# A three-layer block network on one core: tiles placed a round ahead, the modulation in five pieces over three layers, delta masks made with the update

## The reference

```python
for l in range(2):                                   # layers 0 and 1
    shift, scale, gate = split(silu(c) @ w_ada[l] + b_ada[l], 3)     # the modulation, 2048 x 6144
    h = rms_norm(x, norm_g[l]) * (1 + scale) + shift
    u, z_s, q, k, v, z_a = split(h @ w_in[l])        # 6 x 1024 columns
    y_s = s5_mixer(u, ...) * silu(z_s)               # 64 groups of 64 complex states, a scan over time
    y_a = diff_attention(rope(q), rope(k), v, ...) * silu(z_a)       # 8 heads of two maps
    x = x + gate * (concat(y_s, y_a) @ w_out[l])
x = rms_norm(x, final_g)
# layer 2
shift, scale, gate = split(silu(c_2) @ w_ada_2 + b_ada_2, 3)
h = rms_norm(x, norm_gain_2) * (1 + scale) + shift
q_a, k_a, v_a, z_a, b_a, a_a, q_b, k_b, v_b, z_b, gl_a, gl_b = split(h @ w_in_2)
q_a, k_a, v_a = silu(conv4(q_a, k_a, v_a))           # q_a, k_a then of unit length per head
o_a = gated_delta_rule_chunked(q_a, k_a, v_a, g(a_a), sigmoid(b_a))  # 8 heads, chunks of 64 tokens
o_b = sliding_window_attention(q_b, k_b, v_b, ...)   # 16 heads, window 128
mixed = sigmoid(gl_a) * (o_a' @ w_branch_gdn) + sigmoid(gl_b) * (o_b' @ w_branch_swa)
out = x + gate * (mixed @ w_out_2)
```

## Time and profile before

| | us |
|---|---|
| median of 3 runs (lowest, highest) | 4688.14 (4687.24, 4689.46) |
| the profiled execution's own time | 4688.89 |
| its span in the profile | 4687.1 |
| TensorE busy in it | 4429.2 |
| VectorE, ScalarE, GpSimd busy | 1940.2, 818.5, 484.1 |

### The profile page before, as it was taken

One profiled execution on the slowest core, in us unless ns is written; L12 is line 12 of the kernel. 1 busy time (PEld: TensorE's weight loads), 2 busy tenths in 40 slices (PEclk: granted clock), 3 DMA queues, 4 the chain that ended last, 5 costly groups with the idle time before them and its releaser, 6 DMA issues.

```text
span 4687.1 us, 34250 instructions
## 1 busy us (share of the span) xinstructions
PE 4429.2 (94%) x13238; PEld 2253.4 (48%) x13238; DVE 1940.2 (41%) x3496; ACT 818.5 (17%) x1384; POOL 484.1 (10%) x802
## 2 busy tenths in 40 slices
PE   7898899999889989999999899989899999999999
PEld 3454444444436545444444355555555554444444
DVE  4555535664543454356545535151514223321100
ACT  1122201231002221011300212120211013330000
POOL 0122211111321231101022000000000000000000
PEclk8999999999999999999999989999999999999999
DMA  8422233335472222322357321211121222223332
GB/s 295 171 90 74 92 109 104 115 120 169 151 239 79 86 72 83 110 88 68 108 190 233 127 81 36 69 49 59 47 70 48 92 72 68 67 88 128 99 103 76
DMA packets 366736, 495.17 MB, mean 106 GB/s; under 512 B 43899, under 2 KB 277870, under 8 KB 365550
## 3 DMA queue, kind: packets, MB, share of 16 engines
q1 hardware_dynamic: 288112, 340.16, 22.1%
q0 software_dynamic: 37632, 122.71, 8.2%
q10 hardware_dynamic: 40830, 30.11, 2.0%
HBM read 460.42 MB, written 32.51 MB: 105 GB/s over the span
## 4 chain that ended last, share of the span: by engine, by line
PE 75%; DVE 13%; DMA 6%; ACT 2%; issue 2%; ACTq 1%; POOL 0%; DVEq 0%; SPq 0%; POOLq 0%
PE bank L108 73%; DMA side<-in_w_ada 5%; DVE tring L123 4%; DVE tring L117 2%; PE bank L111 2%; ACT tring L114 1%; ACTq L147 1%; DVE tring L132 1%; DVE tring L120 1%; DVE CA L117 1%; DVE SS L117 1%; DVE tring L144 1%; DVE tb L117 1%; DVE dring L120 0%; ACT Est L114 0%
## 5 line engine op out<-in xcount | busy, mean ns | idle before, releaser
L108 PE MATMUL bank<-region_b,wring 128*128 128x512 f32 x4160 | 1872.5, 601 | 9.7 <-ACT region_b L114 9.7
L108 PEld LDWEIGHTS bank<-region_b,wring 128*128 128x128 f32 x4160 | 780.6, 193 | 904.6 <-issue 895.9
L108 PE MATMUL bank<-region_a,wring 128*128 128x512 f32 x2048 | 914.1, 601 | 10.8 <-DMA wring<-in_w_out 10.8
L108 PEld LDWEIGHTS bank<-region_a,wring 128*128 128x128 f32 x2048 | 387.8, 193 | 475.1 <-issue 473.7
L123 DVE SCALAR_TENSOR_TENSOR tring<-side,cact,tring 128x512 f32<-128x512 f32 x420 | 343.2, 817 | 218.1 <-DMA side<-in_w_ada 184.2
L147 POOL DMA_DIRECT2D side<-in_w_ada x448 | 242.8, 542 | 1499.2 <-DVE tring L123 976.5
L114 ACT ACT_TABLE_LOAD x196 | 251.5, 1283 | 437.9 <-DVE sring L120 285.4
L108 PE MATMUL bank<-wring,region_b 128*128 128x512 f32 (+2 forms) x768 | 285.4, 527 | 0.0
L132 DVE RECIPROCAL tring<-tring 128x512 f32<-128x512 f32 x54 | 180.7, 3348 | 134.1 <-ACT tring L114 134.0
L108 PE MATMUL bank<-wring,region_a 128*128 128x512 f32 x512 | 226.4, 600 | 5.9 <-ACT region_a L114 5.9
L108 PE MATMUL bank<-yaT,wring 128*128 128x512 f32 x512 | 227.3, 597 | 0.0
(11 more groups left out here) (237 smaller groups left out, 3320.7 us busy)
## 6 DMA issues: line engine op xcount, KB each, us to landing
wring<-in_w_in SPq DMA_DIRECT2D x180, 1024.0 KB, 5.2
side<-in_w_ada POOLq DMA_DIRECT2D x448, 256.0 KB, 3.2
wring<-in_w_out SPq DMA_DIRECT2D x48, 1024.0 KB, 7.4
yaT<-in_w_ada SPq DMA_DIRECT2D x16, 1024.0 KB, 7.2
wring<-in_w_glu SPq DMA_DIRECT2D x16, 1024.0 KB, 7.8
tring<-x_saved SPq DMA_DIRECT2D x48, 256.0 KB, 3.6
SS<-in_w_ada SPq DMA_DIRECT2D x8, 1024.0 KB, 8.3
side<-in_w_ada SPq DMA_DIRECT2D x8, 1024.0 KB, 9.1
```

Source lines behind the costliest of these rows:

```text
L108: return self.e.matmul(*a, **k) if self.e else self
```

## The change

1. `e_place` of round k+1 is written ahead of `scan` of round k, and `bc_place` of round k into round k instead of k+1.
2. The modulation is five pieces: gate of layer 0, shift and scale of layer 1, gate of layer 1, shift and scale of layer 2, and gate of layer 2, the last beside the window attention of layer 2 through four slots of its own (`gring`). The rates of `carry` go from 1.0, 1.5 and 4 (layer 0) and 0.5, 0.8 and 4 (layer 1) in the three stages of a layer to 1.25, 1.7 and 1.8 in both, and 1.6 in the window attention; `finish_behind` leaves 3 and 2 pieces in layer 0, and 1 and 0 in layer 1.
3. In `state_space_params(1)` two more steps pass between the fetch and the first use.
4. The delta rule's mask for n+1 is made right after the update of n, and one step more lies before n = 1. The separate VectorE step `d_lo` is gone.
5. The convolution has two input tiles (`raws`) instead of one, and its second half, `conv_rest`, is a step later than its first; the unit chain starts a step later still.
6. `ba` is one tile with its 16 columns as weights: 16 matmuls with 512 tokens, a copy on ScalarE, four turns, and the gates made from the turned tile in one instruction each.
7. In the last layer each four channel tiles of the output are turned, copied and stored as soon as they are made (`leave`): 16 stores of 256 KB instead of four of 1 MB.

```diff
@@ -527,7 +530,11 @@
-        mods = [(0, [SHIFT, SCALE]), (0, [GATE]), (1, [SHIFT, SCALE, GATE]), (2, [SHIFT, SCALE, GATE])]
+        mods = [(0, [SHIFT, SCALE]), (0, [GATE]), (1, [SHIFT, SCALE]), (1, [GATE]), (2, [SHIFT, SCALE]), (2, [GATE])]
+        GATE_OF = [1, 3, 5]
...
+        def ada_slots(m):
+            return wide_slots if m == GATE_OF[2] else mslots
...
@@ -704,7 +711,8 @@
-            yield
+            for _ in range(3 if l else 1):
+                yield
...
@@ -728,10 +736,8 @@
             for k in range(NK + 1):
-                if k < NK:
+                if k == 0:
                     do("e_place", l, k)
-                if k:
-                    do("bc_place", l, k - 1)
                 yield
...
@@ -757,6 +763,9 @@
                     aux.give("y", l, k - 1)
+                if k < NK:
+                    do("bc_place", l, k)
+                if k:
                     yield
...
@@ -765,6 +774,8 @@
                     aux.give("y_turn", l, k - 1)
+                if k < NK - 1:
+                    do("e_place", l, k + 1)
                 if k < NK:
...
@@ -879,6 +890,18 @@
+        def leave(k0):
...
+            yield
+            for j in range(TT):
+                aux.take("o_turn", j, k0)
+                do("o_turn", j, k0)
+                aux.give("o_turn", j, k0)
+                if j % 2:
+                    yield
+            for j in range(TT):
+                do("o_store", j, k0)
...
@@ -888,14 +911,14 @@
-                    return None
+                    return leave(n + j - 3) if l == 2 and (n + j) % 4 == 3 else None
...
-            carried[0] = [1.0, 0.5][l]
+            carried[0] = 1.25
...
@@ -911,7 +934,7 @@
-                behind.extend([modulation(1), modulation(2), modulation(3)])
+                behind.extend([modulation(m) for m in range(1, 5)])
...
@@ -920,13 +943,13 @@
-            carried[0] = [1.5, 0.8][l]
+            carried[0] = 1.7
...
-            finish_behind(2 - l)
-            carried[0] = 4
+            finish_behind(3 - 2 * l)
+            carried[0] = 1.8
...
@@ -934,7 +957,7 @@
-            finish_behind(1 - l)
+            finish_behind(2 - 2 * l)
...
@@ -956,15 +979,14 @@
-            def unit():
+            yield
+            do("conv_rest", h0, which, j)
+            yield
+            if which < 2:
...
-                temps.give("conv", h0, which, j)
...
-            if which < 2:
-                return unit()
...
-            return None
...
@@ -1152,7 +1175,12 @@
-        run_all(dense(layer_dense(2, w_two, OFF["ba"], "keep_ba", tokens="blocks", n=2 * GH)))
+        temps.take("ba")
+        run_all(dense(layer_dense(2, w_two, OFF["ba"], "keep_ba", n=2 * GH)))
+        aux.take("ba_turn")
+        do("ba_turn")
+        aux.give("ba_turn")
+        temps.give("ba")
...
@@ -1165,19 +1193,17 @@
+        behind.append(modulation(GATE_OF[2]))
+        carried[0] = 1.6
...
+        finish_behind(0)
...
+        do("fence", "mixed")
...
-        do("fence", "end")
-        for j in range(TT):
-            for k0 in range(0, KT, 4):
-                aux.take("o_turn", j, k0)
-                do("o_turn", j, k0)
-                aux.give("o_turn", j, k0)
-            do("o_store", j)
+        run_all(settle())
...
@@ -2149,17 +2186,20 @@
-                dve.memset(raw[:, 0:3], 0.0).then_inc(*delta_d.up("raw"))
+                dve.memset(raws[:, :, 0:3], 0.0).then_inc(*delta_d.up("raw"))
...
-                c, acc = HT * which + h0 + j, temps.at("conv", h0, which, j)
+                c, acc, raw = HT * which + h0 + j, temps.at("conv", h0, which, j), raws[:, j, :]
...
-                for i in range(1, 4):
-                    own()
-                    dve.scalar_tensor_tensor(acc, raw[:, i:i + T], convw[:, i, c:c + 1], acc, M, AD).then_inc(
-                        *(taken_d.up("conv", h0, which, j) if i == 3 else d_step.up()))
+                stt(acc, raw[:, 1:1 + T], convw[:, 1, c:c + 1], acc, M, AD)
...
+            def conv_rest(h0, which, j):
+                c, acc, raw = HT * which + h0 + j, temps.at("conv", h0, which, j), raws[:, j, :]
+                stt(acc, raw[:, 2:2 + T], convw[:, 2, c:c + 1], acc, M, AD)
+                own()
+                dve.scalar_tensor_tensor(acc, raw[:, 3:3 + T], convw[:, 3, c:c + 1], acc, M, AD).then_inc(*taken_d.up("conv", h0, which, j))
...
@@ -2251,11 +2291,7 @@
-            def d_lo(h, n):
-                if n > 1:
-                    dve.wait_ge(*delta_full.of("dm", h, n - 1))
-                join(h, n)
+                join(h, 1)
...
@@ -2265,6 +2301,8 @@
                 aux.leave(("d_dt", h, n), dve.mine())
+                if n < 5:
+                    join(h, n + 1)
...
@@ -2701,8 +2739,16 @@
+                room(temps.clear("ba"))
...
-                act.activation(gates[:, 1, j, :], banks.at(jid, j)[:, 0:GH], ACT.Sigmoid).then_inc(*taken_a.up("ba", j))
+                act.activation(temps.at("ba")[0:2 * GH, :], banks.at(jid, j)[0:2 * GH, :], ACT.Copy).then_inc(*taken_a.up("ba_tile"))
+                banks.leave((jid, j), act.mine())
...
+            def ba_turn():
+                bank = aux.at("ba_turn")[:, 0:2 * GH * TT].rearrange("p (j h) -> p j h", j=TT)
+                act.wait_ge(*turned.of("ba"))
+                act.activation(gates[:, 1, :, :], bank[:, :, 0:GH], ACT.Sigmoid).then_inc(*taken_a.up("ba"))
+                aux.leave(("ba_turn",), act.mine())
...
@@ -2717,12 +2763,14 @@
-                prev = (h0, which, j - 1) if j else (h0, which - 1, 1) if which else (h0 - 2, 2, 1)
+                prev = (h0, which - 1, j) if which else (h0 - 2, 2, j)
...
-                act.activation(raw[:, 3:T + 3], banks.at(jid, j)[:, :], ACT.Copy).then_inc(*delta_a.up("raw", h0, which, j))
+                act.activation(raws[:, j, 3:T + 3], banks.at(jid, j)[:, :], ACT.Copy).then_inc(*delta_a.up("raw", h0, which, j))
...
+            def conv_rest(h0, which, j):
...
@@ -2997,11 +3045,10 @@
-            def o_store(j):
+            def o_store(j, k0):
...
-                for k0 in range(0, KT, 4):
-                    sp.wait_ge(*(taken_a if k0 % 8 else taken_d).of("o", j, k0))
-                sp.dma_start(out[0, j * P:(j + 1) * P, :], row).then_inc(*out_stored.landing(j))
+                sp.wait_ge(*(taken_a if j % 2 else taken_d).of("o", j, k0))
+                sp.dma_start(out[0, j * P:(j + 1) * P, k0 * P:(k0 + 4) * P], row[:, k0 * P:(k0 + 4) * P]).then_inc(*out_stored.landing(j, k0))
...

```

More of the change, by code:

```diff
@@ L315, in build @@
         band, k2, q2 = sb("band", [P, 16, 256], two), sb("k2", [P, 2, T], two), sb("q2", [P, 2, T], two)
+        gring = sb("gring", [P, 4, T], two)
         two.close()
@@ L324, in build @@
         wslots, mslots = Room([wring[:, i, :, :] for i in range(4)]), Room([mring[:, i, :, :] for i in range(3)])
+        wide_slots = Room([gring[:, i, :].unsqueeze(1) for i in range(4)])
         temps = Room([tring[:, i, :] for i in range(NTEMP)])
@@ L337, in build @@
         ada_in = [sem(f"ada_in{i}") for i in range(3)]
+        late_ada_in = [sem(f"late_ada_in{i}") for i in range(4)]
         first_in = [sem(f"first_ada_in{i}") for i in range(4)]
@@ L503, in fetch @@
                     c = todo.pop(0)
-                    mslots.take("ada", m, *c)
+                    ada_slots(m).take("ada", m, *c)
                     do("ada_fetch", m, *c)
-            for _ in range(len(mslots.places)):
+            for _ in range(len(ada_slots(m).places)):
                 fetch()
@@ L1456, in band_ @@
                           stop=True).then_inc(*scored.up("band", h))
+            def ba_turn():
+                bank, ba = aux.at("ba_turn"), temps.at("ba")
+                room(aux.clear("ba_turn"))
+                pe.wait_ge(*taken_a.of("ba_tile"))
+                for j in range(TT):
+                    i = pe.transpose(bank[:, 2 * GH * j:2 * GH * (j + 1)], ba[0:2 * GH, J[j]], ident[0:2 * GH, 0:2 * GH])
+                i.then_inc(*turned.up("ba"))
+                temps.leave(("ba",), pe.mine())
             def gate_sums():
```

55 lines of the change are left out of this document (29 added, 26 removed).

## The result

The changed kernel takes 4568.01 us (median of 4, 4566.52 to 4569.43), the one before 4688.39 (4 runs, 4687.24 to 4689.46): the ratio is 0.9744, with a 95% interval of 0.973 to 0.9758. It is faster by 120 us, where 177 were forecast, and it lies 18 us outside the range of 4475 to 4550.

A forecast was written before the change was run, and what follows sets the result against it. TensorE was taken to set the time, with savings from its idle time and clock. Terms 80 + 42 + 8 + 20 + 29 + 2 - 1 - 3 = 177 us off gave 4511 us against the 4688.1 median; range 4475 to 4550.

The forecast's parts named there:

- The step that failed: Window attention of layer 2: 64 modulation sums beside it, mostly covered by TensorE's work, cost 1 us (0 to 8).
- rival (d): State space and attention: the modulation's DMA waits move onto the path with 333 sums; 4690 us or more; chance 0.03.
- state space: State-space stages: 14 of 16 waits for `Est` go, 62 us, plus 18 of clock; 80 us (60 to 91).
- output products of both layers, less the rate's cost: Output stages gain 42 and 8 us, mainly from waits tied to modulation's pace; attention loses 3 to the rate.
- opening of layer 2: Opening of layer 2: wide `ba` saves 11 us, waits and clock the rest; 20 us (6 to 26).
- delta rule: Delta rule: masks directly after updates cut TensorE's waits, with 5 us of clock; 29 us (10 to 50).
- end: Kernel's end: turns only move, but fewer bytes remain after the last store; 2 us (0 to 4).
- (a): State space: `Em` takes the place of `Est` and half the gain is lost; 4551 us; chance 0.13.
- the share of the clock: State space: 18 us taken from the low clock's cost, out of up to 29.0 us.
- (b): Delta rule gains only 10 us because convolution and reciprocal were the cause and stay; 4530 us; chance 0.10.
- (e): Whole kernel: no change, the waits only changing names; chance 0.01.
- (c): Whole kernel: everything named is hidden, clock included; 4480 us; chance 0.13.

The follow-up runs named there:

- e1: The changed kernel with the pacing counter set to zero when the last modulation is put behind the window attention: 4499.78 us.
- e3: The e1 kernel with E, B and C placed where they were before the change: 4597.89 us.
- e4: The kernel before with only one edit, E, B and C placed a round ahead: 4603.70 us.
- e6: The e1 kernel with the modulation's three rates as before the change, five pieces and later parameters kept: 4536.41 us.
- e8: The e1 kernel with `ba` computed as before the change, 64 matmuls with 16 columns: 4521.33 us.
- e11: The e1 kernel with the convolution's four taps in one piece as before the change, the two input tiles kept: 4505.78 us.
- e5: The e1 kernel with the delta merges' masks made at the head of the next merge, as before the change: 4533.92 us.
- e7: The e1 kernel with all 16 turns of the output at the end and no store before, stores still 256 KB: 4501.83 us.
- e12: The e1 kernel with the delta rule's first mask and first difference made right behind the product they mask: 4482.48 us.

## Why the prediction was wrong

**The step that failed** is the one on the last modulation, "64 sums of 0.8 us, 52 us, to VectorE's 126 of 385, where TensorE waits 1.5 in all: costs 1 (0 to 8)". It took the 64 sums as spread over the stage and priced only how far TensorE's work covers them. It did not count them out step by step, as it did for layer 0's output products, and did not ask what the counter held after the stretch in which `behind` was empty. It cost 68.2 us by e1. The cover was judged rightly: with the debt taken away this part of the kernel takes 1 us more than before, and twice the sums cost 5.4 us. What was missing was a look at where in the order the 64 sums stand: that alone shows them at one place. The signs of being wrong named waits in the window attention, but no rival had them there; rival (d), sums whose DMA waits lie on the path, was right in kind (1.07 us a sum against its 0.55) and wrong in place.

**The rest of the sum.** Without the failed step the forecast of 4511 was 11 us too high, and inside its range: e1 gives 4499.8. By terms:

| term | forecast (bounds) | measured |
|---|---|---|
| state space | 80 (60 to 91) | 98.1 (e3), 83.6 alone (e4) |
| output products of both layers, less the rate's cost | 42 + 8 - 3 | 36.6 for the rates alone (e6) |
| opening of layer 2 | 20 (6 to 26) | 21.5 for `ba` (e8), 6.0 for the convolution, here and in the delta rule (e11) |
| delta rule | 29 (10 to 50) | 34.1 for the masks (e5) |
| end | 2 (0 to 4) | 2.1 (e7) |
| modulation beside the window attention | -1 (-8 to 0) | -68.2 (e1) |

Each measured figure is a difference of two medians, with some 5 to 10 us of uncertainty by the intervals of the ratios. Taken by the ratios to the kernel before, which ran beside each, they would be 96 (e3), 85 (e4), 34 (e6), 24 (e8), 8 (e11), 31 (e5), 5 (e7) and -66 (e1). The parts of e3, e5, e6, e7, e8 and e11 add up to 198.4, the whole without the debt is 4687.4 - 4499.8 = 187.6. That one part missing makes the others' waits longer is seen in e3 and e5; the 11 us between the two sums are no more than the noise of six differences.

The gain of a stage, which is what the forecast priced, is better read from the stage's own length. From the first to the last turn of `Est` it is 319.6 us before and 270.9 now in layer 0, 321.9 and 288.9 in layer 1: 81.7 less, where 80 were forecast. Layer 0's output products are 49.4 shorter (42 forecast), although the wait for the state-space parameters, forecast as gone, is still 3.72 us of 9.59. The delta rule is 23.5 shorter, where 29 were forecast; in its first three pairs 24.1 us of idle time stay (738 us less 713.92) where 16 were left. So the good sum without the debt is in part luck: the delta rule's term was too high and layer 0's too low.

**State space**: the mechanism was right, `Est` waits in two places only, as forecast, and no wait for `Em` came up, so (a) is out. The size was off in the share of the clock: 18 us were taken of 29, and 28.9 of busy time went (e3 against e1; 26.5 in e4 against the kernel before). **The clock** in all: from before to e1 TensorE's busy time falls by 66.7 us and its idle time by 123.5 (190.2 in spans); 45 were forecast for the clock. The rule of the Trainium skill (TensorE: Matmul & The Clock Gate, Part 1), less than 1% for the ramp, which would have given 4540, pointed the wrong way. e8 has as many records of TensorE as the kernel before, 13238, and the same products, and is busy for 51.8 us less (4377.4 against 4429.2): the kernel before lost at least that, 1.1% of its span, and more, since e8 is not at the full clock throughout. The upper bound, busy time by (1 - clock), is 87 us for the changed kernel, 1.9% of its span, and 44 us, 1.0%, for e12.

**`ba`** ran in four groups of 3.61 us, 14.4 in all, at a clock of 1.00, as forecast. **Delta rule**: the waits at the masks of the merges are down to 0.9 us at most, and what stayed is not the second head's first merge so much as the mask before `d_first`, up to 5.6 us, of which the prediction did not speak. It came with the change: 5.3 us before, 19.0 now. **VectorE's waits for the modulation's DMA** did not go to zero, 51.9 us in 18 waits from 184.2 in 102, and 18.4 in 34 more in the burst. Of the 51.9, 38.5 are in the two stages of output products, where no wait of TensorE is for a sum. TensorE's busy time is below 4400, as forecast. (b) is out by the stage's 23.5 us, and (e) by every part. Without the debt the kernel lies between the forecast and (c), at 4499.8 between 4511 and 4480.

## What to carry to other kernels

A counter that paces background work by steps keeps counting while there is nothing to pace. Whoever appends work later must reset it, or the rate set beside it means nothing; so before such work is called hidden, look at where its instructions stand in the order, not at the rate. Work with a serial chain behind it (four slots, 3.2 us a fetch) costs about 1 us in all when 64 pieces are spread at one in 5 us, and its full 1.07 us a piece in one place. The gain of taking a copy out from behind a chain grows with what else is put into that chain, here by some 6 us of waits. And a run with one part taken out sizes that part in the company of the others, not what the stage gained over the kernel before (34.1 and 23.5 us for the delta rule): for that, measure the stage's length in both kernels.

## What the runs showed of the hardware that was not expected

TensorE was granted the lower clock while it was busy without a gap: 23.00 us busy of 23.00 at 0.50, with 106 records of 128x16 (e8), after a stretch of short matmuls with waits of 2.84 and 2.03 us between them. For 22.52 of those 23 us TensorE was also loading weights (105 loads), so what the profile counts as busy was mostly loads with 16 columns behind each. The eight 128x512 records right behind them took 6.52 us, where eight take 3.70 at the full clock (2558.66 in the changed kernel), and the products after these are at the higher level again. The same work with 512 tokens a matmul ran at 1.00, with 39.14 us busy of 40, but the clock had not fallen before it. So a busy share near 1 does not by itself bring the higher level back in this kernel; what brings it was not measured. After the long waits of the burst the lower level stayed only briefly: in the changed kernel 16 records took 8.51 us at 3719.53, and 7.03 where no wait stands before them.
